# Tokens in three column parts, norm vectors turned apart, the down bias loaded earlier, a quarter of the pick on GpSimd

## The chip, the cores and the metric

The kernel runs on one core of a Trainium2 chip. The metric is device time in microseconds, from one launch to its end; the median of three runs of the kernel before is 1027.93 us (1027.42 to 1028.03). Everything is float32 but for a few small bfloat16 masks.

## The reference

One encoder block over 256 tokens of width 1024. A root-mean-square norm (gain `norm1_g`) feeds one input projection `w_in` (1024 x 2048) whose columns are q, k, v (512 each, eight heads of 64) and the pooling input u (512). Stick-breaking attention over the past keys gives the first half of a mix, normed per head with `sb_norm_g`; trailing means over 2, 4, 8 and 16 frames minus the frame itself, mapped per group by `w_pool` and scaled by `pool_scale`, give the second half. `w_out` (1024 x 1024) brings the mix back and is added to x. Then the mixture of experts:

```python
h2 = rms_norm(x, norm2_g)
logits = h2 @ w_router + b_router          # 32 experts, the top 4 of each token, softmax over them
gu = xb @ w_gate_up[e] + b_gate_up[e]      # 1024 x 2048 for each expert
gate = min(gu[:, :1024], 7); up = clip(gu[:, 1024:], -7, 7)
y = ((up + 1) * gate * sigmoid(1.702 * gate)) @ w_down[e] + b_down[e]
x = x + sum over the 4 experts of softmax weight * y
out = rms_norm(x, final_norm_g)
```

Each expert has 12.6 MB of weights, the 32 of them 403 MB; all are read once.

## The kernel before

**Prologue.** The two token tiles of 128 rows go to `xres`, one DMA each (L377). TensorE (L1344 on) warms up with eight matmuls on a tile of ones, then turns (transposes) the eight 128-column blocks of each tile into PSUM banks 4 to 7 (`turn`, L1375). `norm1_g`, `sb_norm_g` and `pool_scale` are loaded to the rows of one tile `vecs` and turned together (L1365) to `vecT`, whose columns are `G1`, `SBG` and `PSC`; `norm2_g` is loaded as four rows (`g2rows`, L589) and turned in front of the fifth step of the projection (`turn_g2`, L1367) to `G2`. VectorE (`first_half`, L870) and ScalarE (L597) multiply the turned tokens by `G1` into `hT`. The projection loop (L1399) then takes eight steps, one for each 128 rows of `w_in`, and in each multiplies eight column blocks of q and k; `w_qk` comes in eight chunks of 512 KB, each with a semaphore of its own. The roots of the norm are made by ScalarE from the squares of the tokens (L603, L606) and spread over the partitions by two matmuls (`spread_roots`, L1385) before step 6. Behind its root work ScalarE issues the loads of `w_pool`, the router, the router bias and the final gain (L609 to L614). VectorE scales the router by `G2` (L952) after it has moved q and k out and before the softplus work of attention (L916). TensorE then goes through v, scores, u, values, the pooled groups and the output projection in one fixed order written out by hand.

**Experts.** `ring` holds 16 chunks of 1 MB, `area`, `late` and `wide` some more. The sync engine's queue (SP) loads x, `w_in` and `w_out`, then the expert weights, each load waiting until its place is free (`free_first`, L410, then counts of `chunks_used`). Experts go in pairs, each on 64 token slots. The ranks of the tokens in their experts give the pick matrix (`pick_scaled`, L1069): for the first pair VectorE writes four pieces of 128 rows x 64 columns, one for each token tile and expert, into `pick`, which lies on the attention masks `masks[:, 0:256]`. TensorE gathers tokens by it (L1662). The down biases of all experts (`bdown`, in the router's place) are loaded by ScalarE's queue after the last logits (L726) and are used by `add_b_down` (L1666) during the first pair's down projection.

GpSimd makes constants at the start and the windowed sums of the pooling (L576), and nothing later.

## Time and profile before

| | |
|---|---|
| median of 3 runs | 1027.93 us |
| lowest and highest | 1027.42 and 1028.03 us |
| span of the profiled execution, first to last instruction | 1026.2 us |
| TensorE busy | 978.7 us (95%) |
| VectorE, ScalarE, GpSimd busy | 215.3, 104.8, 8.5 us |
| mean DMA rate | 408 GB/s, 418.51 MB |
| TensorE's granted clock | 0.998 of full speed |

The profiled execution has no device time of its own beside its span; the median of the runs stands 1.7 us above the span. In the rows below L is a line of the kernel; L1349 is the matmul helper, so groups there are told apart by the tiles. A float32 matmul shows as two records, a transpose as one. "x" behind a row is a count. DMA share is the mean busy share of the 16 DMA engines.

### The profile page before, as it was taken

The numbers are of one execution on the slowest core, as the hardware profiler recorded it, in microseconds if no ns is written. First come the engines' busy times: TensorE is split into PE (matmuls) and PEld (weight loads), VectorE is DVE, ScalarE is ACT, GpSimd is POOL, SyncE is SP. The second block draws the span as 40 slices with busy tenths as digits, with TensorE's granted clock in tenths as the row PEclk, the third lists the DMA queues.
The fourth block names the chain that finished last, engine by engine and source line by source line (L and its number), as shares of the span: only waits on it lengthen the run. The fifth ranks groups of instructions, "written<-read, shape, count | busy, mean of one in ns | idle before, by whom it ended". The sixth has DMA issues, their size and how long they took to land.

```text
span 1026.2 us, 11169 instructions
## 1 busy us (share of the span) xinstructions
PE 978.7 (95%) x4610; PEld 418.4 (41%) x4610; DVE 215.3 (21%) x472; ACT 104.8 (10%) x181; POOL 8.5 (1%) x27
## 2 busy tenths in 40 slices
PE   9999999999999999899999999999999989898996
PEld 7685534343434333333434343433334333332432
DVE  2234423121121211121212112121112121120121
ACT  2251200000000000000000000000000000000102
POOL 0010000000000000000000000000000000000000
PEclk9999999999999999999999999999999999999999
DMA  9967799999999999999999999999999999999995
GB/s 337 420 274 291 266 383 427 429 428 429 428 429 429 429 429 427 428 427 426 429 429 429 429 429 429 427 429 429 428 428 429 428 427 429 429 429 427 427 426 215
DMA packets 35392, 418.51 MB, mean 408 GB/s; under 512 B 4364, under 2 KB 5032, under 8 KB 10152
## 3 DMA queue, kind: packets, MB, share of 16 engines
q1 hardware_dynamic: 33584, 417.09, 96.7%
q10 hardware_dynamic: 1784, 1.08, 0.4%
q8 instruction: 18, 0.29, 0.1%
q14 instruction: 6, 0.05, 0.0%
HBM read 417.10 MB, written 1.05 MB: 407 GB/s over the span
## 4 chain that ended last, share of the span: by engine, by line
PE 69%; DMA 25%; DVE 3%; issue 2%; ACT 1%; SPq 0%; DVEq 0%; ACTq 0%
PE bank L1349 56%; DMA ring<-in_w_gate_up_dram 13%; PE acc L1349 12%; DMA ring<-in_w_down_dram 12%; DVE area L1160 1%; DVE area L1157 1%; PE bank L1751 1%; DVE area L1096 1%; DMA ring<-in_w_in_dram 1%; ACT wpool L745 1%; DVE sel L858 0%; DVE area L1164 0%; ACT late L819 0%; PE bank L1582 0%; DVE masks L1073 0%
## 5 line engine op out<-in xcount | busy, mean ns | idle before, releaser
L1349 PE MATMUL bank<-ring,area 128*64 128x512 f32 (+1 forms) x1832 | 411.5, 594 | 13.4 <-DMA ring<-in_w_gate_up_dram 13.4
L1349 PEld LDWEIGHTS bank<-ring,area 128*64 128x64 f32 (+1 forms) x1832 | 132.1, 138 | 283.9 <-issue 254.1
L1349 PE MATMUL bank<-ring,wpool 128*64 128x512 f32 x864 | 192.3, 596 | 11.4 <-DMA ring<-in_w_down_dram 6.6
L1154 DVE TENSOR_SCALAR area<-bank 128x512 f32<-128x512 f32 x31 | 21.4, 692 | 444.2 <-PE bank L1349 444.2
L1349 PEld LDWEIGHTS bank<-ring,wpool 128*64 128x64 f32 x864 | 59.8, 137 | 123.9 <-issue 107.9
L741 ACT ACTIVATE bank<-area 128x512 f32<-128x512 f32 x32 | 19.2, 602 | 495.2 <-DVE area L1154 495.2
L1349 PE MATMUL bank<-masks,xres 128*128 128x128 f32 x492 | 66.0, 287 | 2.1 <-DVE masks L1073 0.3
L1349 PEld LDWEIGHTS bank<-masks,xres 128*128 128x128 f32 x492 | 60.4, 196 | 17.7 <-issue 16.6
L1178 DVE COPY wide<-bank 64x512 f32<-64x512 f32 x30 | 20.8, 694 | 198.9 <-PE bank L1349 192.6
L1349 PE MATMUL acc<-wide,masks 128*128 128x512 f32 x120 | 55.5, 606 | 0.0
L1349 PE MATMUL bank<-area 128*64 128x512 f32 (+2 forms) x228 | 47.0, 559 | 0.6 <-DVE area L931 0.5
L750 ACT ACTIVATE wide<-bank 64x512 f32<-64x512 f32 x30 | 17.7, 589 | 243.0 <-PE bank L1349 243.0
L1349 PE MATMUL bank<-bias,sel 64*128 64x512 f32 x124 | 36.9, 641 | 0.0
L1349 PEld LDWEIGHTS acc<-wide,masks 128*128 128x128 f32 x120 | 21.6, 190 | 33.7 <-issue 33.7
L1751 PE MATMUL bank<-ident,area 128*128 128x128 f32 x128 | 22.2, 296 | 10.8 <-DVE area L1164 10.8
L1349 PE MATMUL acc<-area,ring 128*128 128x256 f32 x128 | 28.3, 381 | 0.5 <-DMA ring<-in_w_in_dram 0.5
L1349 PEld LDWEIGHTS bank<-area 128*64 128x64 f32 x228 | 15.5, 137 | 31.6 <-issue 29.4
L1751 PEld LDWEIGHTS bank<-ident,area 128*128 128x128 f32 x128 | 19.0, 206 | 22.9 <-DVE area L1164 17.6
L1096 DVE TENSOR_TENSOR area<-bank,vecT 128x512 f32<-128x512 f32 x30 | 20.7, 688 | 34.3 <-PE bank L1349 34.3
L745 ACT ACTIVATE wpool<-bank 128x512 f32<-128x512 f32 x30 | 17.9, 597 | 79.1 <-PE bank L1751 79.0
L1349 PEld LDWEIGHTS acc<-area,ring 128*128 128x128 f32 x128 | 24.1, 190 | 3.9 <-DVE area L873 0.7
L1349 PE MATMUL acc<-ring,area 128*64 128x512 f32 (+2 forms) x80 | 24.0, 576 | 0.1
(195 smaller groups left out, 429.1 us busy)
## 6 DMA issues: line engine op xcount, KB each, us to landing
ring<-in_w_gate_up_dram SPq DMA_DIRECT2D x113, 2048.0 KB, 24.5
ring<-in_w_down_dram SPq DMA_DIRECT2D x54, 2048.0 KB, 25.6
area<-in_w_gate_up_dram SPq DMA_DIRECT2D x13, 2048.0 KB, 18.9
late<-in_w_down_dram SPq DMA_DIRECT2D x5, 2048.0 KB, 17.2
ring<-in_w_down_dram SPq DMA_DIRECT2D x6, 1024.0 KB, 41.9
ring<-in_w_in_dram SPq DMA_DIRECT2D x8, 512.0 KB, 9.9
ring<-in_w_in_dram SPq DMA_DIRECT2D x4, 1024.0 KB, 17.1
ring<-in_w_out_dram SPq DMA_DIRECT2D x4, 1024.0 KB, 15.7
```

What stands on the lines that cost most here:

```text
L741: a.activation(BG[:], gatec, ACT.Sigmoid, scale=ALPHA).then_inc(sig_ok, 1)
L745: a.activation(dst, BG[:].rearrange("p (j t) -> p j t", j=4), ACT.Copy).then_inc(hT_c, 1)
L750: a.activation(ypair[lo:lo + SLOTS, 0:HALF], BY[0:SLOTS, :], ACT.Copy).then_inc(y_lo, 1)
L1096: v.tensor_tensor(xT[:, 4 * kh:4 * kh + 4, :], src[:].rearrange("p (k t) -> p k t", k=4), G2[:, 4 * kh:4 * kh + 4].unsqueeze(2).to_broadca ...
L1154: v.tensor_scalar(gatec, gbank[:], LIMIT, None, ALU.min).then_inc(gc, 1)
L1157: v.tensor_scalar(upc, ubank[:], LIMIT, -LIMIT, ALU.min, ALU.max).then_inc(uc, 1)
L1160: v.scalar_tensor_tensor(out=upc, in0=upc, scalar=1.0, in1=gatec, op0=ALU.add, op1=ALU.mult).then_inc(tm, 1)
L1178: v.tensor_copy(ypair[lo:lo + SLOTS, HALF:D], BY[SLOTS:P, :]).then_inc(y_hi, 1)
L1349: return t.matmul(o, l, r, start=start, stop=stop, skip_group_check=True)
L1751: m = t.transpose(BG[:, j * P:(j + 1) * P], upc[:, j::4], ident[:])
```

## The change

- The tokens are loaded as three column parts for both tiles at once, of 2, 2 and 4 blocks of 128 columns. The first weight chunk of q and k comes as two halves after the first part, the second part and the second chunk follow, then the third part and the rest. Chunks 2 and 3, 4 and 5, 6 and 7 share a semaphore and are waited for in pairs.
- TensorE warms up with four matmuls, turns `norm1_g`, warms up with three more and turns blocks 0 and 1. Blocks 2 and 3 are turned before step 1, blocks 4 to 7 before step 2. ScalarE copies `G1` out and takes blocks 1, 4, 5 and 7, VectorE blocks 0, 2, 3 and 6, each for all 256 tokens.
- `sb_norm_g` and `pool_scale` are loaded by ScalarE's queue behind the router bias and turned before step 6. `norm2_g` is no longer turned: one DMA writes it to `G2` in pieces of two numbers, behind the final gain's; both wait for that transpose.
- The down biases are loaded to a staging place on the masks (`bstage`) when the last sums over the masks are done, ahead of the gate biases; GpSimd copies them into the router's place after the last logits.
- Counts of the semaphore `tr` and of `tr_a` are renumbered where the turns no longer use them (left out below, as the new semaphores are).
- VectorE writes three of the four pieces of the first pick, GpSimd the fourth; both wait for GpSimd's copy.

```diff
@@ -192,7 +192,6 @@
-        g2rows = part(7744, 2 * P)[0:4, :]
@@ -233,6 +232,8 @@
         lparts = masks[:, 2 * P:3 * P]
+        bstage = masks[:, 0:2 * P]
         stack = sb("stack", [P, NE])
...
@@ -368,16 +371,39 @@
+        def qk_sem(k):
+            return k if k < 2 else 1 + k // 2
         block = ctx.enter_context(nc.Block())
+        def first_pick(on, tt, r):
+            return on.tensor_scalar(pick[:, tt, r * SLOTS:(r + 1) * SLOTS], iota[:, 1:SLOTS + 1],
+                                    rank[:, tt, r:r + 1], stat[:, 6 + tt:7 + tt], ALU.is_equal,
+                                    ALU.mult)
...
         def _(sp):
-            for tt in range(TT):
-                sp.dma_start(xres[:, tt, :], x[0, tt * P:(tt + 1) * P, :]).then_inc(x_in[tt], 16)
-            for k in range(KD):
-                sp.dma_start(w_qk[:, k, :], w_in[0, k * P:(k + 1) * P, 0:2 * SBW]).then_inc(
-                    wqk_in[k], 16)
+            def load_x(i):
+                cols = slice(P * X_PARTS[i][0], P * sum(X_PARTS[i]))
+                sp.dma_start(xres[:, :, cols], x[0].rearrange("(t p) d -> p t d", p=P)[:, :, cols]).then_inc(
+                    x_in[i], 16)
+            def load_qk(k, lo=0, n=2 * SBW, done=None):
+                sp.dma_start(w_qk[:, k, lo:lo + n], w_in[0, k * P:(k + 1) * P, lo:lo + n]).then_inc(
+                    wqk_in[qk_sem(k)] if done is None else done, 16)
+            load_x(0)
+            load_qk(0, 0, SBW, wq0_in)
+            load_qk(0, SBW, SBW)
+            load_x(1)
+            load_qk(1)
+            load_x(2)
+            for k in range(2, KD):
+                load_qk(k)
             for w, col, done in ((w_v, 2 * SBW, wv_in), (w_u, 3 * SBW, wu_in)):
@@ -578,25 +604,35 @@
+            pool.wait_ge(bdown_in, 64)
+            pool.wait_ge(lg_ok, 2)
+            g.tensor_copy(bdown, bstage).then_inc(bdown_c, 1)
+            pool.wait_ge(rank_c, 1)
+            pool.wait_ge(bdown_c, 1)
+            pool.wait_ge(rinv, 4)
+            first_pick(g, 1, 1).then_inc(pickp_ok, 1)
...
             a = nc.scalar
-            for i, (src, lo, n) in enumerate(((norm1_g, 0, 8), (sb_norm_g, 8, 4),
-                                              (pool_scale, 12, 4))):
-                v = src[0, :, :] if len(src.shape) == 3 else src.rearrange("l (r c) -> (l r) c", c=P)
-                act.dma_start(vecs[lo:lo + n, :], v).then_inc(vecs_in[i], 16)
-            act.dma_start(g2rows, norm2_g.rearrange("l (r c) -> (l r) c", c=2 * P)).then_inc(vecs_in[3], 16)
+            act.dma_start(vecs[0:8, :], norm1_g.rearrange("l (r c) -> (l r) c", c=P)).then_inc(vecs_in[0], 16)
             act.wait_ge(edge_c, 3)
...
             a.activation(stat[:, 15:16], epsc[:], ACT.Sqrt).then_inc(warm, 1)
+            act.wait_ge(vec_t, 1)
+            a.activation(G1, bank[0][:, 0:8], ACT.Copy).then_inc(vec_c, 1)
+            def turned(k, b, lo, n):
+                act.wait_ge(xt, n)
+                a.activation(hT[:, k, :], bank[b][:, lo:lo + S], ACT.Copy, scale=G1[:, k:k + 1]).then_inc(tr_a, 1)
             act.wait_ge(vec_c, 1)
-            for tt in range(TT):
-                act.wait_ge(tr, 2 * tt + 2)
-                for k in range(4):
-                    a.activation(hT[:, 4 + k, tt * P:(tt + 1) * P],
-                                 bank[5 + 2 * tt][:, k * P:(k + 1) * P], ACT.Copy,
-                                 scale=G1[:, 4 + k:5 + k]).then_inc(tr_a, 1)
+            turned(1, 5, 0, 2)
+            turned(4, 7, 0, 4)
+            turned(5, 7, S, 4)
+            turned(7, 5, S, 6)
@@ -611,7 +647,12 @@
             act.dma_start(brow[:], b_router.broadcast_to([P, NE])).then_inc(brow_in, 16)
+            act.dma_start(vecs[8:12, :], sb_norm_g.rearrange("l (r c) -> (l r) c", c=P)).then_inc(vecs_in[1], 16)
+            act.dma_start(vecs[12:16, :], pool_scale[0, :, :]).then_inc(vecs_in[2], 16)
+            act.wait_ge(vec_t, 2)
             act.dma_start(fg, final_norm_g.rearrange("(r c) -> r c", c=P)).then_inc(fg_in, 16)
+            act.dma_start(G2.rearrange("p (c s) -> p c s", s=2), norm2_g[0].rearrange(
+                "(c p s) -> p c s", p=P, s=2)).then_inc(vecs_in[3], 16)
@@ -650,6 +691,7 @@
+                act.wait_ge(vec_c, 2)
                 act.wait_ge(pool_ok, b + 1)
@@ -691,6 +733,11 @@
+            act.wait_ge(zc_ok, NPAIR)
+            for r in range(4):
+                act.dma_start(bstage[32 * r:32 * (r + 1), :], b_down[0][:, 2 * P * r:2 * P * (r + 1)]).then_inc(
+                    bdown_in, 16)
             act.wait_ge(u_c, 2)
...
@@ -720,11 +767,6 @@
-            act.wait_ge(lg_ok, 2)
-            for r in range(4):
-                act.dma_start(bdown[32 * r:32 * (r + 1), :], b_down[0][:, 2 * P * r:2 * P * (r + 1)]).then_inc(
-                    bdown_in, 16)
@@ -863,31 +905,27 @@
             choose_bias(0)
-            dve.wait_ge(vec_t, 1)
-            v.tensor_copy(vecT[:, 0:16], bank[0][:, 0:16]).then_inc(vec_c, 1)
             dve.wait_ge(vec_c, 1)
-            def first_half(tt, k, n):
-                dve.wait_ge(tr, 2 * tt + 1)
+            def turned(k, b, lo, n, both):
+                dve.wait_ge(xt, n)
                 v.tensor_tensor(
-                    hT[:, k:k + n, tt * P:(tt + 1) * P],
-                    bank[4 + 2 * tt][:, k * P:(k + n) * P].rearrange("p (k t) -> p k t", k=n),
-                    G1[:, k:k + n].unsqueeze(2).to_broadcast([P, n, P]), ALU.mult).then_inc(g1_c, 1)
-            first_half(0, 0, 4)
-            first_half(1, 0, 2)
-            first_half(1, 2, 2)
+                    hT[:, k:k + both, :], bank[b][:, lo:lo + both * S].rearrange("p (k t) -> p k t", k=both),
+                    G1[:, k:k + both].unsqueeze(2).to_broadcast([P, both, S]), ALU.mult).then_inc(g1_c, 1)
+            turned(0, 4, 0, 1, 1)
+            turned(2, 6, 0, 3, 2)
+            turned(6, 4, S, 5, 1)
             for tt in range(TT):
...
                                 ALU.mult).then_inc(spread_ok, 1)
-            dve.wait_ge(vec_t, 2)
-            v.tensor_copy(G2, bank[4][:, 0:8]).then_inc(vec_c, 1)
             dve.wait_ge(roots_ok, 1)
             v.tensor_copy(roots, bank[6][:, 0:S]).then_inc(roots_c, 1)
+            v.tensor_copy(vecT[:, 8:16], bank[6][:, S + 8:S + 16]).then_inc(vec_c, 1)
             dve.wait_ge(roots_c, 1)
@@ -947,7 +985,7 @@
-            dve.wait_ge(vec_c, 2)
+            dve.wait_ge(vecs_in[3], 16)
             dve.wait_ge(wrouter_in, 16)
@@ -978,6 +1016,7 @@
+            dve.wait_ge(vec_c, 2)
             for j in range(NPAIR):
...
@@ -1106,7 +1145,10 @@
             dve.wait_ge(rank_c, 1)
-            pick_scaled(0)
+            dve.wait_ge(bdown_c, 1)
+            for tt, r in ((0, 0), (0, 1), (1, 0)):
+                d = first_pick(v, tt, r)
+            d.then_inc(pickr_ok, 1)
             v.reduce_max(most[:, 0:1], bank[2][0:1, TT * NE:(TT + 1) * NE], AX_X).then_inc(cnt_m, 1)
...
@@ -1354,33 +1396,28 @@
             pe.wait_ge(ones_c, 1)
-            keep_warm(8)
+            keep_warm(4)
             pe.wait_ge(consts, 5)
-            def turn_vecs():
-                for i in range(3):
-                    pe.wait_ge(vecs_in[i], 16)
-                t.transpose(bank[0][:, 0:16], vecs[:], ident[0:16, 0:16]).then_inc(vec_t, 1)
-            def turn_g2():
-                pe.wait_ge(vecs_in[3], 16)
-                for s in range(2):
-                    m = t.transpose(bank[4][:, s:8:2], g2rows[:, s::2], ident[0:4, 0:4])
-                m.then_inc(vec_t, 1)
-            def turn(src, tt, halves=(0, 1), stepped=True):
+            pe.wait_ge(vecs_in[0], 16)
+            t.transpose(bank[0][:, 0:8], vecs[0:8, :], ident[0:8, 0:8]).then_inc(vec_t, 1)
+            keep_warm(3)
+            def turn(src, tt, halves=(0, 1)):
...
                     for k in range(4):
-                        lo = (4 * kh + k) * P
                         m = t.transpose(bank[4 + 2 * tt + kh][:, k * P:(k + 1) * P],
-                                        d_step(src[:, tt, :], 4 * kh + k) if stepped
-                                        else src[:, tt, lo:lo + P], ident[:])
+                                        d_step(src[:, tt, :], 4 * kh + k), ident[:])
                     m.then_inc(tr, 1)
+            def turn_x(k, b, lo, n=1):
+                for i in range(n):
+                    for tt in range(TT):
+                        m = t.transpose(bank[b][:, lo + i * S + tt * P:lo + i * S + (tt + 1) * P],
+                                        xres[:, tt, (k + i) * P:(k + i + 1) * P], ident[:])
+                m.then_inc(xt, 1)
@@ -1390,22 +1427,41 @@
-            for tt in range(TT):
-                pe.wait_ge(x_in[tt], 16)
-                turn(xres, tt, stepped=False)
-                if tt == 0:
-                    turn_vecs()
+            pe.wait_ge(x_in[0], 16)
+            turn_x(0, 4, 0)
+            turn_x(1, 5, 0)
             for k in range(KD):
-                if k < 4 and k % 2 == 0:
-                    pe.wait_ge(g1_c, 2 + k // 2)
+                if k == 0:
+                    pe.wait_ge(g1_c, 1)
+                    pe.wait_ge(wq0_in, 16)
+                if k == 1:
+                    pe.wait_ge(x_in[1], 16)
+                    turn_x(2, 6, 0, 2)
+                    pe.wait_ge(tr_a, 1)
+                if k == 2:
+                    pe.wait_ge(x_in[2], 16)
+                    turn_x(4, 7, 0, 2)
+                    turn_x(6, 4, S)
+                    turn_x(7, 5, S)
+                    pe.wait_ge(g1_c, 2)
                 if k == 4:
-                    turn_g2()
-                    pe.wait_ge(tr_a, 8)
+                    pe.wait_ge(tr_a, 3)
                 if k == 6:
+                    pe.wait_ge(g1_c, 3)
+                    pe.wait_ge(vecs_in[1], 16)
+                    pe.wait_ge(vecs_in[2], 16)
+                    t.transpose(bank[6][:, S:S + 16], vecs[:], ident[0:16, 0:16]).then_inc(vec_t, 1)
                     spread_roots()
-                pe.wait_ge(wqk_in[k], 16)
+                if k == 7:
+                    pe.wait_ge(tr_a, 4)
+                if k == 1:
+                    pe.wait_ge(wqk_in[1], 16)
+                if k > 1 and k % 2 == 0:
+                    pe.wait_ge(wqk_in[qk_sem(k)], 32)
                 for c in range(8):
+                    if k == 0 and c == 4:
+                        pe.wait_ge(wqk_in[0], 16)
                     m = mm(bank[c // 2][:, (c % 2) * S:(c % 2 + 1) * S],
@@ -1414,9 +1470,6 @@
                 for k in steps:
-                    if k == 0:
-                        pe.wait_ge(vec_c, 2)
                     if k == 0:
...
@@ -1660,6 +1713,7 @@
             pe.wait_ge(pickr_ok, 1)
+            pe.wait_ge(pickp_ok, 1)
             gather_first(0, 1, BM, g0_ok)
@@ -1667,7 +1721,7 @@
-                pe.wait_ge(bdown_in, 64)
+                pe.wait_ge(bdown_c, 1)
                 for n, (tt, r) in enumerate(((0, 0), (0, 2), (1, 1), (1, 3), (1, 0), (1, 2), (0, 1), (0, 3))):
```

## Rows read from the trace of the kernel before

**Rows 1.** The page's slices: GB/s that the DMA engines moved, in 40 slices.
```profile
GB/s 337 420 274 291 266 383 427 429 428 429 428 429 429 429 429 427 428 427 426 429 429 429 429 429 429 427 429 429 428 428 429 428 427 429 429 429 427 427 426 215
```

**Rows 2.** Windows: stretch, length, busy us by engine, clock, DMA share, GB/s.
```profile
12.00:14.00 2.00, 2.00 (x11) 1.77 (x10) 0.00 (x0) 0.00 (x0) 0.00 (x0) 1.00 1.04 422
20.00:22.00 2.00, 2.00 (x11) 1.51 (x9) 0.00 (x0) 0.00 (x0) 0.00 (x0) 1.00 1.08 355
68.00:70.00 2.00, 2.00 (x11) 1.74 (x11) 0.00 (x0) 1.97 (x4) 0.00 (x0) 1.00 0.02 4
200.00:400.00 200.00, 193.93 (x924) 76.58 (x922) 36.89 (x70) 13.10 (x22) 0.00 (x0) 1.00 1.01 428
```

**Rows 3.** Chain of waits: start us, us, what ran.
```profile
1.73 5.90 DMA ring<-in_w_in_dram
...
7.77 14.05 PE acc L1349 x64
21.82 0.33 PE bank L1372 x2
...
29.25 0.44 PE bank L1349 x4
...
106.55 0.94 PE bank L1380 x8
...
365.40 25.30 DMA ring<-in_w_down_dram
```

**Rows 4.** Timeline, first 14 us: start, us, engine, line, operation.
```profile
1.13 3.59 PE L1349 MATMUL acc<-ones 128*128 128x512 bf16 x8 [1.13 <-DVE ones L834]
...
4.71 1.33 PE L1380 MATMUL bank<-ident,xres 128*128 128x128 f32 x8
...
8.46 1.10 ACT L603 ACTIVATE late<-xres 128x1024 f32<-128x1024 f32 x1
...
11.07 0.41 ACTq L609 DMA_DIRECT2D wpool<-in_w_pool_dram  x1
...
12.06 0.58 ACTq L613 DMA_DIRECT2D brow<-in_b_router_dram  x1
```

**Rows 5.** DMA issues and us to landing (L379 loads 3-4; L389).
```profile
xres<-in_x_dram SPq DMA_DIRECT2D x2, 512.0 KB, 4.2
...
wpool<-in_w_pool_dram ACTq DMA_DIRECT2D x1, 256.0 KB, 8.8
...
wrouter<-in_w_router_dram ACTq DMA_DIRECT2D x1, 128.0 KB, 11.7
...
brow<-in_b_router_dram ACTq DMA_DIRECT2D x1, 16.0 KB, 13.0
...
DMA to landing us min/median/max: 8.8/9.1/9.5
...
23.97 2.23 SPq L389 DMA_DIRECT2D ring<-in_w_out_dram  x1
...
DMA to landing us min/median/max: 14.9/15.7/17.0
```

**Rows 6.** Timeline, VectorE between 39 and 48 us.
```profile
39.12 0.42 DVE L952 TENSOR_TENSOR wrouter<-wrouter,vecT 128x256 f32<-128x256 f32 x1
...
47.86 1.02 DVE L916 SCALAR_TENSOR_TENSOR area<-acc,area 128x384 f32<-128x384 f32 x2 [7.90 <-ACT area L633]
```

**Rows 7.** Timeline, TensorE, the first product with the down bias.
```profile
161.31 0.71 PE L1349 MATMUL acc<-wrouter,area 32*128 32x256 f32 x8
```

**Rows 8.** Timeline around the first pick, and a GpSimd addition at 63 us.
```profile
63.35 0.61 POOL L576 TENSOR_TENSOR area<-area 128x256 f32<-128x256 f32 x1 [60.26 <-DVE area L907]
...
116.28 1.12 PE L1349 MATMUL bank<-bias,sel 64*128 64x512 f32 x2
...
116.65 0.98 DVE L1073 TENSOR_SCALAR masks<-iota,rank,stat 128x64 f32<-128x64 f32 x4
...
117.69 0.74 PE L1349 MATMUL bank<-masks,xres 128*128 128x128 f32 x4 [0.28 <-DVE masks L1073]
```

24 lines of the change are left out of this document (13 added, 11 removed).

## The prediction

> **What bounds the kernel now.** First the page's strip of what the DMA engines moved [rows 1]: about 429 GB/s from the seventh slice (154 us) to the last but one; most of the 403 MB of expert weights stream in at a flat rate. The windows say the same: 428 GB/s at a DMA share of 1.01 between 200 and 400 us, with TensorE busy for 193.93 of 200 us [rows 2]. Both are nearly full there, and the chain of waits decides: up to 365 us it runs over TensorE, from there long pieces are transfers (25.30 us and more each) [rows 3]. So the end is set by the weight stream, and the only way to end earlier is to let that stream get on earlier. It does not run free before that: between 68 and 70 us the engines moved 4 GB/s [rows 2]. There the queue waits for places in the ring that the prologue's TensorE work releases. In this stretch the chain is TensorE from 7.77 us on almost without a break [rows 3]. Hence the rule of this forecast: a microsecond by which TensorE's prologue moves, wherever the projections of q, k, v and u have not yet been done, is a microsecond of the whole time, in both directions. A transfer that lands earlier without TensorE moving is worth nothing. The span is 1026.2 us and the median of the runs 1027.93 us; 1.7 us lie around the span and I leave them as they are.
>
> **Part 1, the tokens in three column parts.** Now both token tiles (1 MB) and the first 512 KB of weights are in before the first projection matmul: 1.73 + 5.90 = 7.63 us, and the matmul starts at 7.77 [rows 3]. After the change it needs x columns 0 to 255 (0.25 MB) and half a weight chunk (0.25 MB). Today the first token tile of 0.5 MB is in when its transposes start at 4.71, behind eight warming matmuls of 3.59 us [rows 4]; half the bytes, in packets of a quarter the size, I put at 4.2 us, the weight half at 5.1. Seven warming matmuls with the norm transpose between them end near 4.6. Two transposes (0.94 us for eight, so 0.12 each [rows 3]), then VectorE's product of 128x256, 0.42 us (the same shape as the one in rows 6), with the hand-overs: start at 5.5 us instead of 7.77, **-2.25 us**. Bounds: 5.2, where the weight half lands; 6.2, if the norm gains land late and the three warm-up matmuls behind them (3 x 0.45) come after the tokens.
>
> The other twelve of the sixteen transposes no longer hide in the wait for DMA but stand between steps 0 and 1 and before step 2: 12 x 0.94/8 = **+1.41 us**. The two transposes of the second norm's gain go: 0.33 us [rows 3], **-0.33 us**. A step costs 14.05/4 = 3.51 us [rows 3]. Do the weights keep up? Step 1 starts at 5.5 + 3.5 + 0.5 = 9.5; the 1.5 MB it needs are those that landed at 7.6 before, and small packets add under a microsecond (see the packet times below). Step 2 would start at 9.5 + 3.5 + 1.0 = 14.05 and now asks for chunks 2 and 3 together; chunk 3, the fourth load, issued 3 x 0.5 behind the first's 1.73, landed at 3.2 + 9.5 = 12.7 [rows 5], and would land some 0.9 later. It just fits; I charge 0, bound +0.5. Step 6 is then reached at 29.25 - 2.25 + 1.41 - 0.33 = **28.1 us**.
>
> **Part 2, the norm vectors turned apart.** This is where I see the price. Before step 6 TensorE now waits for the attention norm's gains and the pool scales. ScalarE issues them last in a row: behind three column products, two squares and roots, then the loads of w_pool, w_router and b_router. ScalarE can do its last column product only when the transposes before step 2 are done, near 14.0; three products of 0.42 us bring it to 14.8 to 14.9. Today the squares begin at 8.46 and w_pool is issued at 11.07, 2.61 later; b_router's issue runs from 12.06 to 12.64, so the fourth DMA comes 1.6 after w_pool [rows 4]. So w_pool at 17.5 us and the vectors at 19.1.
>
> How long do they take? Today w_pool lands at 11.07 + 8.8 = 19.9, w_router, issued right behind w_pool's 0.41, at 11.5 + 11.7 = 23.2, b_router at 12.06 + 13.0 = 25.1 [rows 4, 5]. 16 KB take 13.0 us where 512 KB of tokens took 4.2: the small loads stand in line behind each other, and each packet of theirs waits for one of the weight queue's. The windows price it: 16 engines x (4096 + 512 bytes) / 422 GB/s = 0.175 us between 12 and 14 us, and 16 x (2048 + 256) / 355 = 0.104 us between 20 and 22 [rows 2]; w_router has 512 packets, 32 an engine, 32 x 0.104 = 3.3 us, just the 23.2 - 19.9 read above. After the change the w_v and w_u loads with their 2 KB packets cover nearly the whole stay, which saves w_pool some 1.2 us (some 16 packets x 0.07): it lands at 17.5 + 7.6 = 25.1, w_router at 28.4, b_router 1.9 later at 30.3, the vectors at **30.5 us**. Upper bound: today's 14.0 us from w_pool's issue to b_router, 31.8; lower: if the vectors were not behind the others at all, 19.1 plus the tokens' 4.2 = 23.3, no wait.
>
> TensorE waits 30.5 - 28.1 = **+2.4 us** (bounds 0 and 3.7), and behind it in its queue is everything: the roots, steps 6 and 7, all projections. The vectors' own transpose adds half of the removed pair, **+0.17**. The roots matmul, at 29.25 today, comes at 30.65: part 1's gain is more than spent.
>
> The second norm's gain comes as 512 packets of 8 bytes, issued behind the vectors' transpose, near 31.5. With 2.8 us of start (w_pool's 8.8 less its packets and about 1.2 us of end) and 32 packets an engine at 0.18 it lands at 41 to 42 us, while w_out still runs (the last w_out load lands at 23.97 + 17.0 = 41.0 [rows 5]). VectorE waits for it where it scaled the router at 39.12; behind that stand three operations, some 1.0 us, and the softplus work that started at 47.86 because of ScalarE [rows 6]. With the shift of 1.4 there are 6 us to spare: 0.
>
> The Trainium skill (DMA: Bandwidth & Descriptors, section Specifications) has a rule against such a load: below 512 bytes a descriptor costs a read-modify-write and line rate is lost. Of the cost per packet the trace shows nothing like it, w_router's 256-byte packets being no slower than their turn in the line; by the rule the gain would land some microseconds later, still inside the 6, so the sum stays and only the chance of the third case below rises a little.
>
> **Part 3, the down bias early.** Its four DMAs go from after the router to 89 us, before the gate bias's, which land later by their issue time; both have until 114 us. TensorE uses the down bias at 161.31 only [rows 7]. The new copy by GpSimd (256 columns; a GpSimd addition of that size takes 0.61 us [rows 8]) runs near 115 us beside VectorE's top-8 work and ends before the pick: 0.
>
> **Part 4, a quarter of the pick by GpSimd.** VectorE makes four pieces in 0.98 us from 116.65, TensorE starts at 117.69 [rows 8]. Without one piece VectorE is ready 0.25 earlier, at 117.38, but TensorE is at its bias matmuls until 116.28 + 1.12 = 117.40, so at most 0.25 is won, **-0.2 us**. GpSimd's piece has a quarter of the columns of the 0.61 us addition, so I take 0.3; even 0.7 would end at 117.4. Bounds -0.25 and +0.3.
>
> The Trainium skill (SBUF — State Buffer, section Who interferes with whom) says that a VectorE operation in its two-port mode, or with two inputs in SBUF, and a GpSimd operation that reads SBUF exclude each other. No row here shows such a pair on this kernel's short operations. By that rule the four pieces run one after the other and the copy can hold up the top-8 chain for up to 0.5 us: the sum would be 0.2 to 0.7 higher.
>
> **Sum.** -2.25 + 1.41 - 0.33 + 2.4 + 0.17 - 0.2 = +1.2 us: **1029.1 us**. 0.2% is 2.06 us and about what can be told from no change, so this reads as no difference that can be measured, on the slow side.
>
> **Rivals.** (B) The vectors do not stall TensorE: they slip past the router loads, or the line moves faster than I worked out. For it: they are two DMAs of 2 KB; against it: b_router, also small, took 13.0 us. Then -2.25 + 1.41 - 0.33 + 0.17 - 0.2 = -1.2: 1026.7 us. (C) The 8-byte load is served too late. It is safe as long as it finds packets of 4 KB beside it. After w_out (40 us) come 8 KB, then 16 KB packets, 16 x 16384 / 428 GB/s = 0.61 us for each of its own. If it starts to be served after 37.3 us instead of 34.3, more than seven packets are left for the 16 KB time and softplus moves by 0.61 for each further one; ten of them are 6 us, on top of the 1.2: 1033 to 1035 us, clearly slower. Against it: the 3 us of room. (D) TensorE starves for w_qk in steps 1 to 3, through the 1 KB packets and the doubled wait: +0.5 to +1.5, but it eats from the same wait for the vectors, so little comes on top: 1029 to 1030 us.
>
> **How the numbers follow.** Forecast 0.60 (its own range 1028.0 to 1030.8, from 29.4 and 31.8 for the vectors and the pick's bounds), B 0.20, C 0.07, D 0.08, the rest 0.05 to either side. Faster than 1025.87: a tenth, from B's lower end and the rest. Slower than 1029.99: C, and the upper fifth of the forecast and D, 0.20. Within: 0.70. The range 1025.9 to 1031.3 takes in B and the forecast whole and leaves out C.
>
> **What would show it.** Right: first projection matmul near 5.5 us; in the chain a transfer into vecs ending near 30.5 us before the roots matmul; the w_v loads unchanged; softplus still released by ScalarE; TensorE's gather about 0.2 us nearer to the rank. Wrong: roots matmul at 28 us with no wait before it (B), or VectorE's router product after 48 us (C). The forecast falls wholly if the stream's time from 200 us to the end does not shift by what the roots matmul shifts.

## The result and the profile after

The changed kernel takes 1032.66 us (median of 5 runs, 1030.02 to 1033.47) against 1027.93 us (5 runs, 1027.41 to 1028.14): a ratio of 1.0038 [1.0027, 1.0049], slower by more than the 0.2% that can be told. The forecast was 1029.1 us with a range up to 1031.3. The profiled execution has a span of 1031.7 us; it is the one that took 1033.47.

The chain of waits of the changed kernel (start us, us, what ran) answers to [rows 3]; L1391 is now the matmul helper:

```profile
2.75 8.16 DMA ring<-in_w_in_dram
...
11.05 3.69 PE acc L1391 x16
...
15.21 1.20 ACT area L629 x3
16.41 1.04 ACT late L639 x2
...
20.84 11.77 DMA vecs<-in_pool_scale_dram
...
32.95 0.64 PE bank L1391 x4
33.59 8.60 PE acc L1391 x32
42.19 3.43 PE bank L1391 x8
...
123.20 0.71 PE bank L1391 x4
```

The timeline of the same run (start, us, engine, line, operation, in brackets the idle time before it and what ended it):

```profile
5.62 4.29 PE L1391 MATMUL acc<-area,ring 128*128 128x256 f32 x16 [0.17 <-DVE area L913]
...
32.75 0.20 PE L1454 MATMUL bank<-ident,vecs 16*128 16x16 f32 x1 [3.32 <-DMA vecs<-in_pool_scale_dram]
...
47.52 0.43 DVE L990 TENSOR_TENSOR wrouter<-wrouter,vecT 128x256 f32<-128x256 f32 x1 [2.73 <-DMA vecT<-in_norm_g_dram]
...
53.44 1.02 DVE L954 SCALAR_TENSOR_TENSOR area<-acc,area 128x384 f32<-128x384 f32 x2 [5.08 <-ACT area L674]
```

Read the starts of TensorE's pieces. The projection begins at 5.62 us instead of 7.77, as forecast. Step 0 takes 4.29 us where a step before took 3.51, though TensorE stands idle nowhere in it. Step 1 begins at 11.05, right when the transfer issued at 2.75 lands (2.75 + 8.16 = 10.91), not at 9.5: TensorE waited 0.69 us for it. TensorE would be at step 6 at 29.43 and stands idle for 3.32 us until `pool_scale` has landed at 20.84 + 11.77 = 32.61. Steps 6 and 7 then take 8.60 us where half of the 14.05 us that four steps took before [rows 3] is 7.0. q and k are done at 42.19 us, against 36.60 in the profile of before: 5.59 later. Nothing gives it back. The gather of the first pick starts at 123.20 instead of 117.69 [rows 8], 5.51 later, and the span is 5.5 longer.

Why is step 0 slow? The groups of its matmuls, first from 5.6 to 6.8 us, then from 6.9 to 9.7 (number, busy us, mean ns of one record):

```profile
L1391 PE MATMUL acc<-area,ring 128*128 128x256 f32 x3 | 1.5, 634 | 0.2 <-DVE area L913 0.2
...
L1391 PE MATMUL acc<-area,ring 128*128 128x256 f32 x14 | 3.3, 386 | 0.0
```

The first three take 634 ns on average, the others 386, and before the change the same matmuls, between 8 and 21 us, took 381. TensorE is slow here, not starved. The eight warming matmuls of before, 3.59 us [rows 4], had shown the same: 0.45 us each, where 0.24 is the price later (below). The profile's windows give a granted clock of 1.00 for these first microseconds and don't show it.

The windows (stretch, length, busy us of PE, PEld, DVE, ACT and POOL, granted clock, DMA share, GB/s) show why two steps took 8.60, and that the stream is the same as in [rows 2]:

```profile
33.00:34.00 1.00, 1.00 (x7) 0.95 (x8) 0.37 (x2) 0.00 (x0) 0.00 (x0) 1.00 1.01 401
34.00:35.00 1.00, 1.00 (x5) 0.80 (x4) 0.12 (x2) 0.00 (x0) 0.00 (x0) 0.56 1.05 418
...
36.00:37.00 1.00, 1.00 (x3) 0.74 (x3) 0.00 (x0) 0.00 (x0) 0.00 (x0) 0.50 1.05 414
...
200.00:400.00 200.00, 194.17 (x926) 76.75 (x924) 36.01 (x69) 12.80 (x22) 0.00 (x0) 1.00 1.01 428
```

In the idle time and in the first microsecond behind it the granted clock is still 1.00. Then, while TensorE is busy for all of each microsecond, it is 0.56 and 0.50 of full speed, the 1.2 GHz level of its two. From 200 to 400 us it is 428 GB/s as before. The page's slices say it for the whole span, against [rows 1]: the same plateau, only what comes before it is less:

```profile
GB/s 323 406 265 251 266 374 431 426 427 429 429 427 429 427 427 428 431 427 429 427 427 428 430 427 429 428 427 428 429 429 429 429 427 427 429 427 427 428 426 211
```

The landings (page: KB, median us from issue; last line: the 8-byte load of the second norm's gain, issued at 33.29) answer to [rows 5]:

```profile
wpool<-in_w_pool_dram ACTq DMA_DIRECT2D x1, 256.0 KB, 9.4
...
wrouter<-in_w_router_dram ACTq DMA_DIRECT2D x1, 128.0 KB, 12.2
...
brow<-in_b_router_dram ACTq DMA_DIRECT2D x1, 16.0 KB, 12.6
...
DMA to landing us min/median/max: 14.2/14.2/14.2
```

### The profile page after: what moved, and what is told of

Read it like the earlier page. It is cut to its first block, busy times and chain, and to the rows that moved or that the text cites. A ratio compares the mean times of both kernels' runs of the same rounds, so it can differ in the third digit from the quotient of the medians.

```text
span 1031.7 us, 11172 instructions
## 1 busy us (share of the span) xinstructions
PE 983.0 (95%) x4608; PEld 421.3 (41%) x4608; DVE 214.9 (21%) x470; ACT 104.5 (10%) x178; POOL 9.5 (1%) x29
## 4 chain that ended last, share of the span: by engine, by line
PE 69%; DMA 24%; DVE 3%; issue 2%; ACT 1%; SPq 0%; ACTq 0%; DVEq 0%
PE bank L1391 58%; DMA ring<-in_w_gate_up_dram 13%; PE acc L1391 10%; DMA ring<-in_w_down_dram 9%; DMA vecs<-in_pool_scale_dram 1%; PE bank L1805 1%; DVE area L1202 1%; DVE area L1199 1%; DMA ring<-in_w_in_dram 1%; ACT wpool L787 1%; DVE area L1206 0%; DVE area L1135 0%; ACT late L639 0%; DVE sel L900 0%; ACT area L629 0%
## 5 line engine op out<-in xcount | busy, mean ns | idle before, releaser
L1391 PE MATMUL bank<-ring,area 128*64 128x512 f32 (+1 forms) x1832 | 411.1, 594 | 13.0 <-DMA ring<-in_w_gate_up_dram 13.0
L1391 PEld LDWEIGHTS bank<-ring,area 128*64 128x64 f32 (+1 forms) x1832 | 132.2, 138 | 283.0 <-issue 254.7
L1391 PE MATMUL bank<-ring,wpool 128*64 128x512 f32 x864 | 194.4, 601 | 9.1 <-ACT wpool L787 4.8
L1196 DVE TENSOR_SCALAR area<-bank 128x512 f32<-128x512 f32 x31 | 21.4, 691 | 443.2 <-PE bank L1391 443.2
L1391 PEld LDWEIGHTS bank<-ring,wpool 128*64 128x64 f32 x864 | 60.3, 138 | 122.8 <-issue 109.8
L1391 PE MATMUL bank<-masks,xres 128*128 128x128 f32 x492 | 67.1, 290 | 1.9
L1391 PEld LDWEIGHTS bank<-masks,xres 128*128 128x128 f32 x492 | 61.4, 199 | 17.5 <-issue 16.6
L1391 PE MATMUL acc<-wide,masks 128*128 128x512 f32 x120 | 55.5, 605 | 0.0
L1391 PE MATMUL bank<-area 128*64 128x512 f32 (+2 forms) x228 | 46.8, 558 | 0.6 <-DVE area L969 0.6
L1391 PE MATMUL bank<-bias,sel 64*128 64x512 f32 x124 | 36.9, 641 | 0.0
L1391 PEld LDWEIGHTS acc<-wide,masks 128*128 128x128 f32 x120 | 21.6, 189 | 33.7 <-issue 33.7
L1391 PE MATMUL acc<-area,ring 128*128 128x256 f32 x128 | 30.7, 402 | 0.9 <-DMA ring<-in_w_in_dram 0.7
L1391 PEld LDWEIGHTS bank<-area 128*64 128x64 f32 x228 | 15.6, 137 | 31.4 <-issue 30.0
L1391 PEld LDWEIGHTS acc<-area,ring 128*128 128x128 f32 x128 | 25.6, 203 | 5.2 <-issue 0.9
L1391 PE MATMUL acc<-ring,area 128*64 128x512 f32 (+2 forms) x80 | 24.0, 576 | 0.2 <-ACT area L697 0.2
```

The costliest lines, as they stand in the source:

```text
L1196: v.tensor_scalar(gatec, gbank[:], LIMIT, None, ALU.min).then_inc(gc, 1)
L1391: return t.matmul(o, l, r, start=start, stop=stop, skip_group_check=True)
```

## The experiments

Each ran beside the kernel before on the same chip. Where nothing else is said the diff is against the changed kernel.

### The vectors' place in the line

The main question is whether the late vectors explain the whole loss. Their two loads go ahead of `w_pool`, all else stays:

```diff
+            act.dma_start(vecs[8:12, :], sb_norm_g...)      # and pool_scale
             act.dma_start(wpool[:], ...)
...
-            act.dma_start(vecs[8:12, :], sb_norm_g...)      # behind brow
```

> The changed kernel with one thing reordered: ScalarE's queue issues the two vector loads (attention norm, pool scale) ahead of w_pool, the router and its bias, not behind them. Theory (small loads stand in line behind each other, one packet of theirs for one of the weight queue's; the vectors pay for the 72 packets an engine ahead of them): issued at 18.9 and 19.2, they land near 23, TensorE reaches step 6 at 29.4 without a wait and its clock stays at full; 3.3 us of wait and 1.7 us of half clock go, the kernel is 5 us faster than the profiled changed one, within 0.5 us of the kernel before (1027.9 to 1028.6). Rival (any load issued at 19 us beside the saturated weight queue lands after some 12 us, whatever stands ahead): the vectors still land near 31, the wait is 1.5 to 2 us and the time 1030 to 1031.

1027.56 us (10 runs, 1026.28 to 1029.69) against 1027.96: 0.9996 [0.9987, 1.0005], 5 us less than the changed kernel. Its chain of waits:

```profile
5.62 3.93 PE acc L1391 x16
...
28.28 0.16 PE bank L1454
28.44 0.64 PE bank L1391 x4
29.08 6.91 PE acc L1391 x32
35.99 3.43 PE bank L1391 x8
```

The trace has the two vectors landed at 22.1 and 22.4 us, 4.4 us behind their issues at 17.70 and 18.04; behind the other three loads it was 11.8 us. Step 6 is reached at 28.28 us, near the 28.1 of the forecast, there is no wait, steps 6 and 7 take 6.91 us, and q and k end at 35.99, which is 0.6 earlier than before; the span is 1025.6, also 0.6 shorter. So this is what the change without its late vectors is worth in a good profile, and two DMAs in the wrong place of a line cost the rest.

It was run again:

> a_vec_first once more, as the version that may beat both, on the same chip as the next three. Theory: 1027.5, 0.3 to 0.5 us faster than the kernel before (the roots matmul came at 28.3 instead of 29.25, of which a longer transpose and roots matmul give 0.35 back), with more spread than before because the early loads land unevenly. Rival: no gain, 1028.

1027.79 us (11 runs) against 1028.17: 1.0000 [0.9991, 1.0009]; the roots matmul at 28.90 us, span 1026.4. The 0.6 is not to be told from nothing.

The other half of the change's part 2, late vectors without the column parts (against the kernel before: `vecs[0:8]` alone is loaded and turned at the start, the rest behind `brow` and before step 6, and `final_norm_g` waits for that turn):

```diff
-                for i in range(3):
-                    pe.wait_ge(vecs_in[i], 16)
-                t.transpose(bank[0][:, 0:16], vecs[:], ...)
+                pe.wait_ge(vecs_in[0], 16)
+                t.transpose(bank[0][:, 0:8], vecs[0:8, :], ...)
...
                 if k == 6:
+                    pe.wait_ge(vecs_in[1], 16)
+                    pe.wait_ge(vecs_in[2], 16)
+                    t.transpose(bank[6][:, S:S + 16], vecs[:], ...)
```

> The kernel before with the late vectors alone: attention norm and pool scale loaded behind the router bias and turned before step 6, as in the change; tokens and weights are loaded and turned as before. Theory (the vectors' wait exists only because part 1 makes ScalarE's squares, and so its loads, 7.8 us later): w_pool is issued at 11.1, the vectors land near 25, before TensorE reaches step 6 at 29; no wait, 1028.0 within 0.3. Rival (putting the vectors behind the router loads is harmful by itself): a wait before the roots matmul and 1030 or more.

1028.11 us (10 runs) against 1027.96: 1.0003 [0.9993, 1.0012].

```profile
29.33 0.16 PE bank L1410
...
30.13 6.91 PE acc L1352 x32
```

No wait stands before the vectors' transpose at 29.33. The late vectors alone cost nothing, for ScalarE's squares begin near 8.5 us there and the loads go out early; and the column parts cost nothing where the vectors don't wait for them (above). Together, part 1 puts ScalarE's last column products behind transposes that end at 15 us (the chain above: products 15.21, squares 16.41), so the vectors' loads, issued at 12.90 and 13.30 us with the late vectors alone, are issued at 20.46 and 20.84, and step 6 asks for them at the same time.

### The clock behind the wait

Eight more matmuls on the tile of ones, put before the wait of step 6, then eighteen:

```diff
                     pe.wait_ge(g1_c, 3)
+                    for _ in range(8):                      # 18 in the second kernel
+                        mm(bank[7][:], ones[:], ...)
```

> The changed kernel with eight more warming matmuls on ones, written to a free bank, ahead of the wait of step 6 (8 x 0.43 = 3.4 us, the length of the wait). It adds work that the output does not need. Theory (the wait costs twice: 3.3 us of idling, and the granted clock that falls to 0.50 behind it for some 3 us, 1.7 us): the vectors land at the same 32.6, the granted clock stays at 1.00, steps 6 and 7 take 6.9 instead of 8.6 us, the roots matmul to the end of q and k is 1.7 us shorter; about 1.7 us faster than the changed kernel in a profiled run with that drop. Rival (the slow steps 6 and 7 come from something else, as weights that land late or the vectors' product): still 8.6 us.

1031.71 us (5 runs) against 1027.96: 1.0035 [1.0022, 1.0049]. Too few were put in:

```profile
29.02 1.89 PE L1391 MATMUL bank<-ones 128*128 128x512 bf16 x8
32.65 0.20 PE L1456 MATMUL bank<-ident,vecs 16*128 16x16 f32 x1 [1.74 <-DMA vecs<-in_pool_scale_dram]
```

Eight of them took 1.89 us, 0.24 each, where the eight at the start took 3.59 [rows 4]; 1.74 us of idle time were left, and the clock still fell (0.52, 0.50, 0.50 and 0.78 in 34 to 38 us, steps 6 and 7 again 8.60). By that price the array runs at its lower level, 1.2 GHz, at the start, and here it was at 2.4: I had sized the filler by the wrong row. With eighteen:

> The test that c_warm_wait was meant to be: there eight warming matmuls ran for 1.89 us only (0.24 each), 1.74 us of wait were left and the granted clock fell all the same. Now eighteen of them (18 x 0.22 = 4.0 us), work that the output does not need, so that TensorE has no idle time before step 6. Theory (the idle time brings the clock down): the granted clock stays at 1.00 from 33 to 38 us and steps 6 and 7 take 6.9, not 8.6 us; even with some 0.4 us of matmuls beyond the landing the kernel is 1.2 us or more faster than the changed one: 1030 to 1031.5. Rival (the clock falls at this place whatever TensorE does, or steps 6 and 7 are slow for another reason): 8.6 us again and a time of 1032 to 1034.

```profile
29.28 3.88 PE bank L1391 x18
...
33.97 6.91 PE acc L1391 x32
```

The filler leaves no idle time, the granted clock stays at 1.00 and steps 6 and 7 take 6.91 us, although the roots matmul is no earlier (33.33 against 32.95). So the fall hangs on the idle time, not on the work behind it, and it costs 8.60 - 6.91 = 1.7 us. In the profiles q and k end at 40.88 us instead of 42.19: 1.3 earlier, where 1.7 less the some 0.5 by which the filler overran the landing are 1.2. The time is 1031.75 us (10 runs) against 1027.80, 1.0033 [1.0023, 1.0042]. That is 1.1 us under the ten runs of the changed kernel taken together (below; median 1032.85), but those spread over 6 us, so the times alone would not show it.

Not every wait of this size does it. In the kernel that holds the later loads back (below) TensorE stood for 1.69 us in front of step 2:

```profile
16.38 14.05 PE L1392 MATMUL acc<-area,ring 128*128 128x256 f32 x64 [1.69 <-DMA ring<-in_w_in_dram]
```

The four steps behind it took 14.05 us, the full-clock price [rows 3], and the granted clock stayed at 1.00. What tells this wait from the one of 1.74 us is not shown.

The Trainium skill (TensorE: Matmul & The Clock Gate, Part 1) has the array fall back to half speed when it has been idle and return after sustained work; the traces of the wait at step 6 agree: 3.32 or 1.74 us of idle time, then 0.50, then 1.00 again; the wait of 1.69 us had no such fall behind it.

### The wait moved behind the projection

TensorE no longer waits at step 6; the vectors are turned behind step 7:

```diff
@@ if k == 6
-                    pe.wait_ge(vecs_in[1], 16)
-                    pe.wait_ge(vecs_in[2], 16)
-                    t.transpose(bank[6][:, S:S + 16], vecs[:], ...)
@@ behind m.then_inc(qk_ok, 1)
+            pe.wait_ge(vecs_in[1], 16)
+            pe.wait_ge(vecs_in[2], 16)
+            t.transpose(bank[7][:, 0:16], vecs[:], ...)
```

> The changed kernel with the wait for the two vectors and their transpose moved behind step 7; the roots matmul stays before step 6 without that wait; the loads stay where the change put them, behind the router bias. Theory (the landing at 32.6 is too late only for its place in TensorE's queue): TensorE does the 7 us of steps 6 and 7 meanwhile, which reach past 36; no wait is left, no clock drop, and the time is that of a_vec_first, 1027.0 to 1028.5. Rival (late small loads hurt by something else too, for example the second norm's gain, issued after them and landing near 50 when issued at 37, so that VectorE is late for softplus at 47): 1030 or more.

1038.88 us (4 runs) against 1027.80: 1.0099 [1.0072, 1.0126]. My theory fell and the rival held. The roots matmul is at 28.82 and q and k end at 36.17, and yet the kernel is 6 us slower than the changed one:

```profile
36.10 0.23 PE L1469 MATMUL bank<-ident,vecs 16*128 16x16 f32 x1
...
36.68 0.40 ACTq L654 DMA_DIRECT2D vecT<-in_norm_g_dram  x1
...
58.11 0.42 DVE L991 TENSOR_TENSOR wrouter<-wrouter,vecT 128x256 f32<-128x256 f32 x1 [19.27 <-DMA vecT<-in_norm_g_dram]
...
60.73 1.65 PE L1392 MATMUL acc<-area,masks 128*128 128x256 f32 x4 [8.76 <-DVE area L958]
```

The 8-byte load is issued at 36.68, 3.4 us later than in the changed kernel, and takes 21.41 us instead of 14.2. VectorE stands 19.27 us at the router's product and TensorE 8.76 us behind VectorE's softplus work; the span is 1036.8, 10.6 longer than before. The clock falls behind this wait too: it is 0.50 in the windows from 56 to 65 us and 0.82 in the next, which makes TensorE's work from 60.73 on some 2.3 us longer. With q and k 0.4 earlier, -0.4 + 8.8 + 2.3 = 10.7 us account for the 10.6. This is rival C of the prediction. Its price fits: 32 packets an engine, each behind one of 16 KB at 0.61 us, are 19.5 us, with the 2.8 us of start 22.3, a little over the 21.41. It is an upper estimate, as the first of them still stood beside smaller packets.

### Parts 3 and 4 alone

Against the kernel before: the down bias through `bstage`, GpSimd's copy and its quarter of the pick:

```diff
+            g.tensor_copy(bdown, bstage).then_inc(bdown_c, 1)
...
+            first_pick(g, 1, 1).then_inc(pickp_ok, 1)
...
-            pick_scaled(0)
+            dve.wait_ge(bdown_c, 1)
+            for tt, r in ((0, 0), (0, 1), (1, 0)):
+                d = first_pick(v, tt, r)
```

> The kernel before with parts 3 and 4 of the change alone: the down bias early over the masks with GpSimd's copy, and the fourth piece of the first pick on GpSimd. The head of the kernel is untouched. Theory: TensorE's gather starts 0.2 us sooner behind the ranks, nothing else moves: 1027.7, -0.2 us. Rival (VectorE and GpSimd exclude each other on the copy and on the pick): no gain, up to +0.5: 1027.9 to 1028.4.

1027.95 us (11 runs) against 1027.96: 1.0004 [0.9994, 1.0013]. The timeline around the pick:

```profile
115.03 0.25 DVE L1039 SCALAR_TENSOR_TENSOR wpool<-acc,stat,brow 128x32 f32<-128x32 f32 x1 [0.75 <-PE acc L1369]
115.04 0.40 POOL L590 COPY wrouter<-masks 128x256 f32<-128x256 f32 x1 [31.80 <-PE acc L1369]
115.31 0.20 DVE L1043 MAX8 wpool<-wpool 128x8 f32<-128x32 f32 x1
...
116.79 0.76 DVE L376 TENSOR_SCALAR masks<-iota,rank,stat 128x64 f32<-128x64 f32 x3
116.86 0.63 POOL L376 TENSOR_SCALAR masks<-iota,rank,stat 128x64 f32<-128x64 f32 x1 [1.42 <-DVE rank L1121]
...
117.63 0.71 PE L1369 MATMUL bank<-masks,xres 128*128 128x128 f32 x4
```

VectorE writes three pieces in 0.76 us (four took 0.98 before [rows 8]) and TensorE gathers at 117.63 instead of 117.69; from the operation that gives the ranks to the gather it is 1.10 us against 1.30, so 0.2 are won there and mostly lost again by a start that was 0.13 later. GpSimd's piece takes 0.63 us, not the 0.3 that I took; it still ends before TensorE can use it.

The Trainium skill (SBUF — State Buffer, section Who interferes with whom) has a VectorE operation with two inputs in SBUF, or in its two-port mode, and a GpSimd operation that reads SBUF shut each other out. This trace does not show it for VectorE: its three pieces took 302 to 314 ns each beside GpSimd's, where the four of before took 305 to 314 with GpSimd idle. Whether they run in the two-port mode no row tells, and no run has GpSimd's piece alone, so whether its 0.63 us hold a delay stays open. Beside GpSimd's copy of 0.40 us VectorE's operations took 0.25 and 0.20 us as in the kernel before, but they read one tensor each from SBUF, so the part of the rule on two inputs says nothing about them.

### Is the early start worth anything?

Three ways to begin, each with the vectors out of the way. Chunk 1 ahead of the second token part, and all twelve transposes before step 2:

```diff
-            load_x(1)
             load_qk(1)
+            load_x(1)
```

> a_vec_first with the second weight chunk loaded ahead of the second column part of the tokens, and the four transposes of that part moved from before step 1 to before step 2. Theory (step 1 waits in some runs for chunk 1, which landed at 10.9 in the changed kernel's profile, 9.75 in a_vec_first's, and this sets the spread of the runs): chunk 1 lands 0.5 to 1 us earlier, step 1 starts at 9.6, the twelve transposes stand together; 0 to 0.5 us faster in the median than a_vec_first and a narrower spread. Rival (the early loads are slow by their small packets and the order does not matter; the products of ScalarE and VectorE behind the twelve transposes come late for step 2): same or 0.5 slower.

1028.84 us (10 runs) against 1027.80: 1.0007 [0.9998, 1.0017]. The second half of chunk 0 landed at 1.80 + 7.17 = 8.97 us and held up step 0 for 0.74 us, so the roots matmul came at 29.93; no gain, as the rival said. That the new order made this half late isn't shown: in the kernel with eighteen fillers, whose first loads are those of the changed kernel, the same half held step 0 up until 8.65.

The tokens as two whole tiles, as before, but turned in between the steps:

```diff
-                sp.dma_start(xres[:, :, cols], ...)
+                sp.dma_start(xres[:, i, :], x[0, i * P:(i + 1) * P, :]).then_inc(x_in[i], 16)
```

> a_vec_first with the tokens loaded as before the change, two whole tiles of 4 KB packets ahead of all weights, while their transposes stay where the change put them, twelve of them between the steps. Theory (part 1 buys its early start and pays with transposes in line): the first projection matmul starts at 6.8 instead of 5.6, everything behind it is 1.2 us later, 1028.7. Rival (the start is given back at chunk 1 anyway, which is in sooner behind large packets): same as a_vec_first.

1030.15 us (10 runs) against 1027.80: 1.0041 [1.0016, 1.0065], worse than expected:

```profile
1.24 4.72 DMA xres<-in_x_dram
...
7.35 4.88 PE acc L1388 x16
```

The column parts are worth 7.35 - 5.62 = 1.7 us of start. Step 0 took another 0.9 us more (4.88 us against 3.93 with the vectors first), and not for want of weights, as TensorE is idle nowhere in it. Its matmuls from 7.4 to 9.7 us, then from 9.9 to 12:

```profile
L1388 PE MATMUL acc<-area,ring 128*128 128x256 f32 x6 | 2.7, 626 | 0.2 <-DVE area L910 0.2
...
L1388 PE MATMUL acc<-area,ring 128*128 128x256 f32 x11 | 2.6, 383 | 0.0
```

Until 9.7 us they run at the slow price. TensorE had stood idle for 1.16 us before the tokens came, which the kernel with the vectors first does not do.

All vectors loaded at the start, as before, and the column parts kept:

```diff
             act.dma_start(vecs[0:8, :], norm1_g...)
+            act.dma_start(vecs[8:12, :], sb_norm_g...)      # and pool_scale
```

> The changed kernel with the two vectors loaded at the very start, right behind the first norm's gain, which leaves part 1 as it is. Theory (only the landing after 28 us mattered): no wait, same as a_vec_first, 1027.2 to 1028. Rival (two more small loads in the first microseconds push the first tokens and weights back): 0.3 to 1 us slower than a_again.

1027.48 us (11 runs, 1026.63 to 1028.49) against 1028.17: 0.9993 [0.9984, 1.0002]. It is the lowest median of all, and not to be told from before.

```profile
1.81 6.65 DMA ring<-in_w_in_dram
...
8.51 1.99 PE acc L1391 x8
```

In this profile the whole early start is given back (roots matmul at 29.42 us, 29.25 before): the second half of chunk 0 lands at 8.46 us, and TensorE, done with the first half of step 0, waits for it. But it is the profile of one of the slower runs, 1028.27 us.

### Why the first weights land late

In the kernel before, 422 GB/s were moved at 4 to 5 us, and 287, 238 and 246 in the three microseconds from 6 on. In the changed kernel 170, 150, 229, 269 and 262 were moved from 4 to 9 us, just when the first weights are due. Two attempts at it, both against the kernel with all vectors at the start. SP issues nothing behind chunk 1 until chunk 0 is in:

```diff
             load_x(2)
+            sp.wait_ge(wqk_in[0], 16)
             for k in range(2, KD):
```

> i_vec_start (the changed kernel with all norm vectors loaded at the start) with one wait added on the sync queue: the weight chunks 2 and on are issued only when chunk 0 has landed whole. Theory (the first chunks are late because the issues behind them compete for making or moving packets): chunk 0's second half and chunk 1 land 1 us earlier than the 8.5 and 10.4 of i_vec_start's profile, step 1 starts at 9.6, and the time is 0.5 to 1 us below i_vec_start. Rival (the slow stretch from 4 to 9 us belongs to the first reads of w_in themselves, as it stands in the kernel before at 6 to 9 us): chunk 1 as late as ever, chunks 2 and 3 later still, 0 to 2 us slower than i_vec_start.

1028.41 us (11 runs) against 1027.67: 1.0004 [0.9995, 1.0013]. The half chunk landed at 7.15 us, 1.3 earlier, but it lands between 5.95 and 8.61 us in the eight profiles with the changed kernel's first loads, so one profile doesn't show that the wait did it. Chunks 2 and 3 landed only at 16.24, and the roots matmul came at 30.59. Then the tokens on ScalarE's queue, beside SP's weights:

```diff
-            load_x(0)                                       # SP; x parts 1 and 2 too
+            load_x(0)                                       # ScalarE, ahead of norm1_g
```

> i_vec_start with the three column parts of the tokens issued by ScalarE's queue, around the first norm's gain, and only the weights by the sync queue. Theory (the engines lack packets in the first microseconds, busy share 0.59 to 0.8 between 4 and 6 us in the changed kernel, because one queue issues all): two queues fill them, the first half of chunk 0 lands with the first tokens, chunk 1 by 9.5, and it is 0.5 to 1 us faster than i_vec_start, 1026.5 to 1027.2, faster than the kernel before. Rival (ScalarE's issues delay its own table load and the gain's landing, or taking turns packet by packet holds the first tokens back to 4.8 us): the first matmul at 6 us or later and no gain.

1030.34 us (10 runs) against 1027.67: 1.0023 [1.0013, 1.0032]. `norm1_g` came at 5.0 us and the first projection matmul at 7.79; step 0 took 5.55 us, its matmuls at the slow price until 11.4 (633 ns on average). The rate was 411 GB/s at 4 to 5 us, but 262 to 299 from 5 to 7, and with the loads held back 227 to 276 from 4 to 7. A slow stretch stays in both, so it is not made by the loads issued later, nor by one queue for all. It doesn't stand where the weights' loads begin either: in the last kernel these were the first to be issued, and it came after 411 GB/s. Its cause stays open.

### The changed kernel again

> The changed kernel itself, a second profile and more times beside a_again. Its runs lay in two groups, 1030.0 to 1030.7 and 1032.7 to 1033.5. Theory (what differs is when the first weight chunks land, by 1 us, and whether the clock falls behind the wait, 1.7 us): the median stays 1032 to 1033, 4 to 5 us above a_again, and a profile in the lower group shows a full clock from 33 to 38 us or chunk 1 in by 9.8. Rival: the groups come from the weight stream after 200 us, with the roots matmul at 33 us in both.

1034.24 us (median of 4: 1030.77, 1033.31, 1035.18, 1035.94) against 1028.17: 1.0064 [1.0049, 1.0080]. The profiled execution is the one of 1030.77, span 1028.9:

```profile
2.75 6.93 DMA ring<-in_w_in_dram
...
9.82 3.69 PE acc L1391 x16
...
19.62 10.84 DMA vecs<-in_pool_scale_dram
...
30.60 0.20 PE L1454 MATMUL bank<-ident,vecs 16*128 16x16 f32 x1 [2.40 <-DMA vecs<-in_pool_scale_dram]
...
30.80 0.64 PE bank L1391 x4
31.44 8.60 PE acc L1391 x32
```

> The changed kernel itself, a third profile, for the same question: theory, the roots matmul at 31.5 to 33 us and its time following that and the clock between 33 and 38 us; rival, the time does not follow them.

One run, 1030.99 us, span 1029.0: step 1 at 9.64, the vectors 19.45 + 10.69 = 30.14 after a wait of 2.25 us, then 31.12 + 8.60.

These two profiles are worth laying beside the forecast. It had step 1 at 9.5 us, step 6 reached at 28.1, a wait of 2.4, the vectors in at 30.5 and the roots matmul at 30.65. They have 9.82 and 9.64, 28.20 and 28.03, 2.40 and 2.25, 30.46 and 30.14, 30.80 and 30.48. Every term is there, and the span is still 2.7 and 2.8 us over that of before instead of 1.2: what is left is the half clock of steps 6 and 7.

So the changed kernel's runs spread over 6 us, where 26 of 28 runs of the kernel before, beside the first four experiments, lay between 1027.24 and 1030.18. In all three profiles of it the clock fell to 0.50 and steps 6 and 7 took 8.60: that is not what differs. What differs is how long step 0 takes at the slow price (4.29 us, then 3.72 and 3.72), when chunk 1 lands (10.91, 9.68 and before 9.64) and, made larger on the way, when the vectors do (32.61, 30.46, 30.14). The runs above 1035 us have no profile. This is an ordering over three profiles, not a proof.

### The law behind the sum

From ten profiles, the end of q and k beside the span (us); in the last four columns the vectors are late:

```
            vec_first  before  vec_again  vec_start  chunk1  whole_x  third  second  warm_wait  changed
q, k end      35.99    36.60    36.45      36.97     37.48   38.52    39.72   40.03    42.09     42.19
span         1025.6   1026.2   1026.4     1026.3    1026.9  1028.1   1029.0  1028.9   1031.3    1031.7
```

Over 6.2 us the span follows one to one; the difference of the two rows is 989.6 before and 988.9 to 990.0 in all ten. In the five other profiles (eighteen fillers, late vectors alone, parts 3 and 4 alone, loads held back, tokens on ScalarE's queue) it is 989.2 to 989.6. The kernel with the wait behind the projection (36.17 and 1036.8) is the exception that says where the law ends: it holds only while what comes behind the projection isn't late by itself.

## Why the prediction was wrong, point by point

In the measured profile three steps failed. The clock behind the wait was no term of the sum (+1.7 us). The weights and the pace of step 0 were put at nothing (+1.3). The wait itself was 3.32 us and not 2.4 (+0.9). The second and third profile of the same kernel have hardly anything of the last two; the missing clock is in all three.

- **The end is set by the prologue.** Right, by the table above.
- **Start at 5.5 us.** Right: 5.62, so 2.15 of the 2.25 us were taken in.
- **"Do the weights keep up? ... I charge 0, bound +0.5."** Wrong for the measured profile, by two things of about the same size. First, step 0 was priced at 3.51 us, the price of a TensorE at full pace, and took 4.29, against 3.72 in the second and third profile: its start was drawn forward to where the matmuls still run slowly, which the 0.45 us of the warming matmuls [rows 4] could have told. Second, chunk 1 held up step 1 for 0.69 us, to 11.05 instead of 9.5. I took the landing of the first 1.5 MB from before and added under a microsecond; that landing had been hidden behind a later start, and it moves by over a microsecond from one execution to the next. Step 6 is reached at 29.43 instead of 28.1: **+1.3**. The second and third profile reached it at 28.20 and 28.03, the kernel with the vectors first at 28.28: the good end of the same spread.
- **Rival D** named the starving and its size, +0.5 to +1.5, and held that the wait for the vectors would swallow it. It did not: the late step 1 moves the transposes, ScalarE's last products and so the vectors' loads by as much, and the wait did not get shorter.
- **The wait for the vectors, 2.4 us with bounds 0 and 3.7.** The mechanism, the waiting instruction and the releasing transfer were right. It took 3.32: **+0.9**. The larger part is that ScalarE was later than I took it, `w_pool` issued at 18.86 instead of 17.5, since its last column products waited for the late transposes. The line itself took 9.4, 12.2 and 12.6 us, where I had 7.6 for the first, as I let 2 KB packets beside it save 1.2 us and nothing was saved; but from `w_pool`'s issue to the last vector it was 13.75 us against my 13.0.
- **The clock.** The term that is missing altogether: **+1.7**, shown by the eighteen matmuls. The two steps behind the wait were sized by their price of before (7.0 us for two), and in all four profiles with a wait at step 6 they took 8.60.
- **Transpose and roots matmul.** 0.2 us more, as the latter took 0.64 instead of 0.44 [rows 3].
- **The sum.** 1.2 + 1.3 + 0.9 + 1.7 + 0.2 = 5.3 us, against 5.5 in the profile. The median is 4.7 above that of before. Of the 3.6 us between the forecast and the median the clock alone is 1.7; with it in the forecast the range would have reached 1033.0 and held the time. The later set's median, 1034.24, lies beyond that too.
- **The second norm's gain.** The landing was wrong (47.5 us, not 41 to 42), the conclusion right: the softplus work is at 53.44, still released by ScalarE, at no cost. Its issue at 33.29 was 1.8 later than I took it, and it took 14.2 us instead of some 10, as when issued at 28.80 (9.6 us): the beginning of rival C, within the room that was there. The other way to place the wait brought rival C in full.
- **Part 3 at nothing, part 4 at -0.2.** Right, as far as it shows: the operation that gives the ranks came 5.70 us later than before, the gather 5.51, so 0.2 were won between. Both are too small to see in the time.
- **Rival B** had the right mechanism for another kernel: with the vectors loaded first its 1026.7 is 0.9 and 1.1 below what was measured.
